# Keeping h in device memory during the expert stage, a fourth slot of first weights, and expert loads asked for at the projection's end

## What is computed

```python
for l in range(2):
    h = h + token_mixer(rms_norm(h, ln1_g[l]), ...)     # w_in, four mixers, gates, w_out
    h = h + hier_moe(rms_norm(h, ln2_g[l]), ...)        # top-1 of 4 groups, top-2 of its 8 experts
return rms_norm(h, final_g)

def expert_block(args):                                 # in hier_moe, for the rows of expert e
    xb, e = args
    hdn = jax.nn.silu(xb @ w1[e]) * (xb @ w3[e])        # 1024 -> 256
    return hdn @ w2[e]                                  # 256 -> 1024
out = zeros.at[slot_tok].add(ys * slot_w[:, None])      # each token: two experts' rows, weighted
```

## Time and profile before

| | |
|---|---|
| median of three runs | 1519.6 us |
| the profiled execution | 1519.7 us, span 1517.9 us |
| TensorE matmul busy | 1386.2 us, 91% |
| VectorE, ScalarE, POOL busy | 429.9, 507.6, 497.8 us |
| moved by DMA | 331.2 MB, mean 218 GB/s |
| expert stage of layer 0, layer 1 | about 500 to 760 us, 1244 to 1505 us |

### The profile page before, as it was taken

The page is one execution under the profiler, slowest core; times in us unless marked ns, Lnnn a source line. Parts: engine busy times, 40 slices in busy tenths (PEclk is TensorE's granted clock), DMA queues, the critical chain, the costliest instruction groups (busy, mean ns, idle before and its releaser), DMA issues.

```text
span 1517.9 us, 18876 instructions
## 1 busy us (share of the span) xinstructions
PE 1386.2 (91%) x7446; PEld 959.0 (63%) x7446; DVE 429.9 (28%) x1025; ACT 507.6 (33%) x845; POOL 497.8 (33%) x247
## 2 busy tenths in 40 slices
PE   5999999999999799777799999999999988988775
PEld 4888877788888433232388888777888873333222
DVE  3232544410213211011443325443112141110116
ACT  4612466632233111111144225665222331111111
POOL 4533333456751111110054342335557311111101
PEclk9999999999999799999899999999999989999998
DMA  6722222234363899999945223222334639999995
GB/s 234 248 84 84 70 70 70 70 97 134 102 233 153 355 414 416 417 416 416 372 163 184 73 67 104 70 70 70 101 137 151 257 144 404 416 416 417 417 406 201
DMA packets 134801, 331.20 MB, mean 218 GB/s; under 512 B 16149, under 2 KB 89925, under 8 KB 116280
## 3 DMA queue, kind: packets, MB, share of 16 engines
q1 hardware_dynamic: 124920, 310.08, 54.0%
q0 software_dynamic: 9792, 19.89, 3.4%
HBM read 312.16 MB, written 33.55 MB: 228 GB/s over the span
## 4 chain that ended last, share of the span: by engine, by line
PE 70%; SPq 17%; DMA 6%; DVE 3%; ACT 2%; issue 1%; POOL 1%; DVEq 0%; POOLq 0%; ACTq 0%
PE ps L515 18%; PE ps L516 17%; PE ps L517 17%; SPq L437 11%; PE ps L854 8%; SPq L431 5%; DMA w<-in_w 4%; PE ps L683 2%; PE ps L663 1%; PE ps L671 1%; PE ps L619 1%; DMA xg<-x_dram,toks 1%; PE ps L772 1%; PE ps L846 1%; DVE ut L1373 1%
## 5 line engine op out<-in xcount | busy, mean ns | idle before, releaser
L515 PE MATMUL ps<-uH,ringH 128*128 128x512 f32 x720 | 282.4, 392 | 0.0
L516 PE MATMUL ps<-uL,ringH 128*128 128x512 f32 x720 | 280.9, 390 | 0.0
L517 PE MATMUL ps<-uH,ringL 128*128 128x512 f32 x720 | 280.7, 390 | 0.0
L854 PE MATMUL ps<-w,xT 128*64 128x512 f32 x1024 | 243.7, 631 | 40.4 <-DMA w<-in_w 37.9
L854 PEld LDWEIGHTS ps<-w,xT 128*64 128x64 f32 x1024 | 82.1, 146 | 198.4 <-issue 196.7
L1251 POOL TENSOR_TENSOR ringL<-raw,ringH 128x2048 fp32r<-128x2048 f32 (+1 forms) x31 | 138.1, 4461 | 129.8 <-ACT ringH L989 129.8
L515 PEld LDWEIGHTS ps<-uH,ringH 128*128 128x128 f32 x720 | 135.6, 188 | 29.1 <-issue 0.7
L517 PEld LDWEIGHTS ps<-uH,ringL 128*128 128x128 f32 x720 | 135.4, 188 | 28.7
L516 PEld LDWEIGHTS ps<-uL,ringH 128*128 128x128 f32 x720 | 135.5, 188 | 27.7
L1299 POOL TENSOR_TENSOR ringL<-raw,ringH 128x2048 fp32r<-128x2048 f32 x32 | 147.2, 4599 | 5.0 <-ACT ringH L1117 5.0
L854 PE MATMUL ps<-w,hT 128*64 128x512 f32 x512 | 118.8, 605 | 32.8 <-ACT hT L1183 29.1
(11 more groups left out here) (252 smaller groups left out, 2059.0 us busy)
## 6 DMA issues: line engine op xcount, KB each, us to landing
w<-in_w SPq DMA_DIRECT2D x188, 1024.0 KB
raw<-in_w_in SPq DMA_DIRECT2D x54, 1024.0 KB, 5.2
y_dram<-attT SPq DMA_DIRECT2D x8, 1024.0 KB, 11.9
braw<-in_w_branch SPq DMA_DIRECT2D x32, 256.0 KB, 4.4
raw<-in_w_out SPq DMA_DIRECT2D x8, 1024.0 KB, 5.2
yb<-y_dram SPq DMA_DIRECT2D x8, 1024.0 KB, 11.4
h_dram<-hs SPq DMA_DIRECT2D x2, 2048.0 KB, 11.2
hs<-h_dram SPq DMA_DIRECT2D x2, 2048.0 KB, 10.5
```

Of the source, the lines that this page charges most:

```text
L515: mm(o, h, rh, start=first, stop=False)
L516: mm(o, h, rl_, start=False, stop=False)
L517: return mm(o, l, rh, start=False, stop=last)
L854: ins = mm(o[r], lhs[:, r], rhs[x], start=first, stop=last, skip_group_check=True)
```

## The change

- **h in device memory.** The even rows of `y_dram` (a token's first choice) are no longer zeroed; POOL writes each row block of `hs` there after its store to `x_dram` (`keep_rows`), the last after two gathers. `out_rows(p)` on VectorE adds, to a slot that holds a first choice, the gathered row `xg`, which is h: `xg * first_choice + product`, with `first_choice` 1 or 0 from the lists. So `y_dram`'s two rows sum to h plus the experts' share, and `sum_rows` is one addition that writes `hs`. `hs` is free meanwhile. ScalarE's copy is gone. There is one `yy`, one `xT` and three `xg`.
- **Slots.** w13 gets a fourth slot, in the places of `hs` and of `R_O`; w2 has five halves of 1 MiB (2.5 pairs). w13 of pair 15 goes to slot 0.
- **Order of loads.** The wait for the stored rows is behind four more loads. w13 is asked for up to two pairs ahead of w2. w2 of pair 15 is loaded like the others, before yb; the next layer's first columns too.
- **The end.** `combine_early` and the two halves of `combine_last` become one, after the last yL, over six banks; row additions go block by block and the norms begin between them.
- **The start.** In layer 0 the transposes of row block 3 stand one half product later.

```diff
-SLOTS, NS = 3, NP - 2
+SLOTS, W2_SLOTS, NS = 4, 5, NP - 2
+LAST = NP - 1
+def w13_slot(p):
+    return (p % SLOTS, p // SLOTS) if p < LAST else (0, LAST // SLOTS + 1)
+def w13_ahead(p):
+    return p + (2 if p < 6 else 1 if p < 11 else 0)
 ...
+           enumerate(((R_U, R_U + 16 * KB), (R_RAW, R_RH), (R_RAW + 16 * KB, R_RH + 16 * KB), (R_T2, R_O)))]
+    w2 = [sb(f"w2_{s}", [P, 2, D], f32, off) for s, off in
+          enumerate((R_B, R_B + 8 * KB, R_T1, R_T1 + 8 * KB, R_T1 + 16 * KB))]
 ...
             hold(sp, bank_filled.h, bank_filled.at(lay, used_at(U_OUT + 3)))
+            w13_half(3, 1)
+            for x in range(2):
+                w13_half(2, x)
+            for x in range(2):
+                w2_half(1, x)
+            hold(sp, plan_kept.h, plan_kept.at(lay, 1))
             hold(sp, u2_stored.h, u2_stored.at(lay, 16 * NT))
-            w13_fill(2)
-            w2_fill(2)
-            hold(sp, plan_kept.h, plan_kept.at(lay, 1))
-            w2_fill(1)
-            for p in range(SLOTS, NP):
-                hold(sp, up_filled.h, up_filled.at(lay, p - SLOTS + 1))
-                w13_fill(p)
-                if p < NP - 1:
-                    hold(sp, down_filled.h, down_filled.at(lay, p - SLOTS + 1))
-                    w2_fill(p)
+            w2_half(2, 0)
+            hold(sp, rows_stored.h, rows_stored.at(lay, 16 * NT))
+            w13_half(3, 0)
+            ahead = SLOTS
+            for p in range(2, NP):
+                while ahead <= min(w13_ahead(p), LAST):
+                    hold(sp, up_filled.h, up_filled.at(lay, (ahead if ahead < LAST else LAST - 3 + SLOTS) - SLOTS + 1))
+                    for x in range(2):
+                        w13_half(ahead, x)
+                    ahead += 1
+                for x in range(2):
+                    if (p, x) != (2, 0):
+                        hold(sp, down_filled.h, down_filled.at(lay, (2 * p + x - W2_SLOTS) // 2 + 1))
+                        w2_half(p, x)
+            if lay + 1 < L:
+                hold(sp, up_filled.h, up_filled.at(lay, NP - 2))
+                sp.dma_start(raw[:, 0, :]..., w_in_cols(lay + 1, COL["gv"], 256))
+            hold(sp, y_stored.h, y_stored.at(lay, 16 * NS))
             for t in range(NT):
                 ...  # yb[t] <- y_dram
 ...
                 pool.dma_start(x_dram[t * P:(t + 1) * P, :], xw[:]).then_inc(u2_stored.h, 16)
+                if t < NT - 1:
+                    keep_rows(t)
 ...
+            gather(0)
+            gather(1)
+            keep_rows(NT - 1)
+            hold(pool, plan_kept.h, plan_kept.at(lay, 1))
+            gather(2)
+            hold(pool, rows_stored.h, rows_stored.at(lay, 16 * NT))
             for p in range(NS):
+                scatter(p)
                 if p + 3 < NP:
                     gather(p + 3)
-                scatter(p)
 ...
+            def out_rows(p):
+                if p:
+                    dve.wait_ge(y_stored.h, y_stored.at(lay, 16 * p))
+                dve.wait_ge(down_filled.h, down_filled.at(lay, p + 1))
+                for c in range(2):
+                    last = v.scalar_tensor_tensor(yy[:, c * 512:(c + 1) * 512].rearrange("p (q k) -> p q k", k=KD),
+                                                  xg[p % 3][:].rearrange("p (k q) -> p q k", k=KD)[:, c * 64:(c + 1) * 64, :], first_choice[:, p:p + 1],
+                                                  bank(A[c]).rearrange("p (q k) -> p q k", k=KD), ALU.mult, ALU.add)
+                last.then_inc(out_ready.h, 1)
```

More of the change, by code:

```diff
@@ L887, in combine_window @@
                     mm(bank((1, A[5])[x % 2]), tok_w[:, tmc(t)], yLw[:, c], start=False, stop=True).then_inc(win_sum, 1)
-            def token_rows(y, c, t, first, last):
-                mm(bank(SUM_BANKS[c][t]), tok_of[y][:, tmc(t)], yH[y][:, c * 512:(c + 1) * 512], start=first, stop=False, skip_group_check=True)
-                return mm(bank(SUM_BANKS[c][t]), tok_of[y][:, tmc(t)], yL[y][:, c * 512:(c + 1) * 512], start=False, stop=last, skip_group_check=True)
-            def combine_early():
-                hold(pe, last_low.h, last_low.at(lay, 1))
-                hold(pe, tokens_ready.h, tokens_ready.at(lay, 1))
-                for t in range(NT):
-                    token_rows(0, 0, t, True, False)
@@ L900, in combine_last @@
-            def combine_last(c):
-                hold(pe, last_low.h, last_low.at(lay, c + 2))
-                hold(pe, tokens_ready.h, tokens_ready.at(lay, 2))
-                for t in range(NT):
-                    if c and t == 2:
-                        hold(pe, half_added.h, half_added.at(lay, NT))
-                    if c:
-                        token_rows(0, c, t, True, False)
-                    token_rows(1, c, t, False, True).then_inc(sum_filled.h, 1)
+            def combine_last():
+                hold(pe, last_low.h, last_low.at(lay, 3))
+                hold(pe, tokens_ready.h, tokens_ready.at(lay, 2))
+                for x in range(2 * NT):
+                    t, c, b = x // 2, slice(x % 2 * 512, (x % 2 + 1) * 512), SUM_BANKS[x % 6]
+                    if x >= 6:
+                        pe.wait_ge(sum_added.h, sum_added.at(lay, x - 5))
+                    for m, (y, w) in enumerate((y, w) for y in range(2) for w in (yH, yL)):
+                        last = mm(bank(b), tok_of[y][:, tmc(t)], w[y][:, c], start=m == 0, stop=m == 3)
+                    last.then_inc(sum_filled.h, 1)
@@ L934, in _ @@
                 pair(p)
-            combine_last(0)
             def window_lists(n):
-                hold(pe, half_added.h, half_added.at(lay, NT))
                 hold(pe, win_slots, n + 1)
@@ L1219, in window_item @@
                 hold(act, win_turned, n + 1)
-                gained(xT[0], range(KD)).then_inc(win_columns, 1)
+                gained(xT, range(KD)).then_inc(win_columns, 1)
                 hold(act, win_up, n + 1)
@@ L1313, in _, with keep_rows @@
                 .then_inc(route_scaled.h, 1)
+            def keep_rows(t):
+                pool.dma_start(y_dram[2 * P * t:2 * P * (t + 1), :].rearrange("(p c) n -> p c n", c=2)[:, 0, :], hs[:, t, :]).then_inc(rows_stored.h, 16)
             for t in range(NT):
@@ L1699, in _ @@
             v.tensor_tensor(dx[:], v8[:, :, 1], v8[:, :, 0], ALU.subtract).then_inc(router_args.h, 1)
-            list_tokens()
+            link(list_tokens())
+            link(v.scalar_tensor_tensor(first_choice[:], tokf[:], 2.0, bank(A[4])[:, 256 + NP:256 + 2 * NP], ALU.mult, ALU.subtract))
+            v.tensor_scalar(first_choice[:], first_choice[:], 1.0 - SENT, None, ALU.add)
             for x in range(2):
```

204 lines of the change are left out of this document (92 added, 112 removed).

## The result

| | before | after |
|---|---|---|
| median (lowest to highest) | 1518.8 us (1517.4 to 1520.8) | 1505.7 us (1503.7 to 1506.9) |
| profiled execution: span | 1517.9 | 1504.9 |
| PE busy | 91% | 92% |
| DMA moved | 331.20 MB | 331.20 MB |

The changed kernel takes 0.9912 of the time before (95% interval 0.9894 to 0.9929), 13.4 us less by that ratio and 13.1 by the two medians. The forecast was 1505.4. Its total was right, but partly by luck: one large term came out at half to two thirds of its size, and something that it did not know of filled part of the gap.

The account below looks back on a forecast made before the run. The expert stage was taken as bound by weight bytes at 417 GB/s, TensorE bounding the rest. 2 x 4.8 + 2.0 + 1.0 + 1.7 = 14.3 us off 1519.7 gave 1505.4; range 1498 to 1517.

Parts of the forecast that it names:

- X: Landing of pair 15's first weights, where its up product starts: before 735.97 and 1481.17, forecast near 729.5 and 1468.
- Earlier loads, 4.8 us a layer: Expert stage: loads start 8.3 us sooner, less 2.5 for bytes and 1.0 for dryness; bounds 0.8 to 6.8.
- I take 2 us late and 1 us more of dryness: Expert stage's start: fourth store delays pair 0 by 2 us (0 to 4), loading queue dry 1 us longer.
- bytes moved into the busy time: Expert stage: fourth row store and keep_rows(3) now run in the full stream, 1.26 us each, costing 2.5 us a layer.
- The start, 1.7: Layer 0's start: TensorE no longer waits for the fourth ut before a product not needing it, 1.7 us (0.8 to 1.7).
- The end of layer 0, 2.0: From X to TensorE's next layer, near X + 32.5 instead of X + 35.4: 2.0 us gained (0 to 4).
- The end of layer 1, 1.0: From X to the last ut, near X + 29.4 instead of X + 30.9: 1.0 us gained (0 to 3).
- Results with h added, nothing: VectorE's two product-and-adds per pair, 0.68 to 1.4 us each, are hidden; the single yy's scatter wait costs nothing.
- rival (d): Slower: the single yy's copy, scatter and wait set the pair pace once landing exceeds 12.8 us, up to 1567; chance 0.06.
- (a): Early loads given back: gather(0) lands 4 us late, refills too; X gains 0.8 to 3 us a layer; 1511 to 1517; chance 0.21.
- (b): More than forecast: no dryness, layer ends give their full 4 and 3 us; 1497 to 1500; chance 0.09.
- (c): Queue fills earlier, then stands until plan_kept and pair 0; ends give nothing; within 3 us of before; chance 0.06.

Follow-up runs that it names:

- before_again: The kernel before, unedited, measured and profiled once more: 1518.0 us, ratio 1.000.
- start_alone: The kernel before with only the layer 0 start edit, row block 3's transposes asked for one product later: 1517.2 us, ratio 0.9989.
- after_again: The changed kernel, unedited, measured and profiled once more: 1505.6 us, ratio 0.9918.
- start_undone: The changed kernel with the layer 0 start edit undone, row block 3's transposes back in their old place: 1507.3 us, ratio 0.9918.
- kept_early: The changed kernel with VectorE's copy of the routing plan moved ahead of rows_copy(0): 1505.5 us, ratio 0.9905.
- wait_back: The changed kernel with the wait for all four row stores put back ahead of the early weight loads: 1513.3 us, ratio 0.9959.
- experiment 5: The same run as kept_early: the changed kernel with VectorE's plan copy ahead of rows_copy(0): 1505.5 us, ratio 0.9905.
- experiment 7: The changed kernel with VectorE's sum_rows(1) moved behind the two last_out_low halves at the layers' ends: 1506.2 us, ratio 0.9912.
- Experiment 11: The changed kernel with the product-and-add of each half of a pair's result done twice, same outcome: 1510.1 us, ratio 0.9943.

## Why the prediction was right, and where it was not

*What bounds the kernel.* Right. The stage moves 415 GB/s throughout its middle, and X moved with the loads. The reading of the earlier trace rows was too wide: slices 13, 19 and 39 of before moved 355, 372 and 201 GB/s; 404 to 417 holds for 14 to 18 and 33 to 38.

*Earlier loads, 4.8 us a layer: mis-sized.* Measured 2.5 and 2.3 in the first pair of profiles; over the executions (before, before_again and start_alone against after, after_again, start_undone and kept_early) 300.0 - 297.1 = 2.9 in layer 0 and 300.7 - 297.1 = 3.5 in layer 1. The 8.3 us of start were right (the loads go out at 484.75, right at the projection's end; 8.0 us before wait_back's). The step that failed is "I take 2 us late and 1 us more of dryness, nearer to the idle store": the store took 9.02 and 9.44 us, outside even the bound of 8.7, pair 0 was 3.4 us late, and the queue moved less than its 415 GB/s by bytes worth 3.6 us. The reason given, that the loads have only just begun when the store goes out, did not help: 5 us after the first request about 2 of the 8.4 MB had passed, and the store shared the engines with the rest. The prediction took the rule of the Trainium skill (DMA: Bandwidth & Descriptors, Queues, rings and completion order) as half of the engines and 1.3 us; the store was 6.0 us late. The trace agrees with the turns themselves, 134 packets of the store to 158 of the loads. But packets half as large get 30.7% of the engines' time, not half, and the 4.1 us until the first of them come on top. The arithmetic of dryness itself held: the text had the bytes last from 491 to 515.6, they lasted from 484.8 to 510. What it overlooked is that plan_kept stands behind rows_copy(0), and so behind the same late gather, and keep_rows(3) as well (experiment 5). The other term of X, 2.5 us for bytes moved into the busy time, is seen by half: keep_rows(3)'s 1.26 us shows as 0.4 and 0.5 in wait_back; no run has the store's 1.26 by itself.

*The start, 1.7.* By A 1.95 between the two profiles once the episode's 3.15 is taken off, 1.4 in the mean: right.

*The end of layer 0, 2.0.* TensorE's next layer starts at X + 32.0 (760.71) against the forecast X + 32.5, ut(0) at X + 25.9 against X + 26.1. In C 1.9 between the two profiles, 2.4 where no episode falls into it. Right; the order of VectorE that the text wrote out is what TensorE waits for (4.43 us), and experiment 7 moved it.

*The end of layer 1, 1.0.* The last ut starts at 1498.40, X + 28.7 (forecast X + 29.4); E is 1.5 shorter, or nothing where pair 15's up product falls to half clock. Within its bounds.

*Results with h added, nothing.* Right for the change as it is: 1.11 us each, between the bounds 0.68 and 1.4, no wait for the scatter, B the same without it. The doubling taken from ScalarE's row was too high for this operation: 1.11 against 0.68 is 1.6 times. The Trainium skill's rule on 16-byte lines (SBUF — State Buffer, Door 1: The DMA port swizzle) agrees with the trace in its direction; no run has the same operation without the stride, the nearest is the norm's scalar_tensor_tensor (L1381), 1.28 us for twice the elements. Experiment 11 shows that the margin is real and small: 2.2 us more a pair and rival (d)'s loop closes, though at 4 us in all and not at 28 times the excess, since it holds VectorE and the scatter, not the loads.

*Not in the sum.* 3.15 us of the 13.0 between the profiles are a half-clock episode that the first profile of before happened to have. Added up from the table: start 1.95, episode 3.15, stages 2.54 and 2.30, ends 1.89 and 1.51, less 0.34 for a later first product: 13.00. The forecast's 14.3 hit by luck: 4.8 us too much for the loads met 3.15 that no view of the change could show. The median of the runs is less exposed to the episode than one profile is, and still gives 12.5 to 13.4 (ratios 0.9912 and 0.9918): the parts of the change alone, by the means, are 1.4 + 2.9 + 2.4 + 3.5 + 0.7 = 10.9. Some 2 us between the two stay unassigned.

*The rivals.* (a) was the closest: its mechanism (the late gather) came in full, at nearly its price for pair 0 (3.4 us of 4), but it took a quarter to half of the gain and not most of it. (b), (c) fell by X; (d) did not come.

## What to carry to other kernels

A request that is moved ahead of a small transfer makes the small one late by what it puts into the queue; ask who waits for it, and whether the next requests wait for that. A head start in a stage bound by bytes is worth only what can be asked for without interruption until the first slot comes free: write down the bytes asked for and the time of the next request, as a chain, before counting the head start as gained. And profile the unchanged kernel twice: here the first profile held 3 us that the second did not, more than most single parts of the change.

## What was unexpected in the hardware's behaviour

A direct store of 0.5 MB issued 5 us after the loads filled the queue took 9.02 and 9.44 us in place of 3.0: its first packet passed 4.1 us after the issue in place of 1.1, and then the two queues' packets took turns, 134 to 158, at half the size. TensorE's clock fell to half at 150 us in one execution of before and not in another, where it was 100% busy in both; and pair 15's up product in layer 1 is partly at half clock in the seven profiles where TensorE had waited 2.75 us or more for it, and in none of the seven with 2.39 or less. And B, C and D of one and the same kernel differ by 0.6 to 1.5 us between executions, so a part of under 1.5 us is read from one profile only with a second beside it.
